# Six reordered places and two shares for GpSimd in a transformer kernel: picks by products at the start of its expert layer

## The chip, the cores and the metric

The kernel runs on one core of a Trainium2 chip, as one program. The metric is the device time of one execution in microseconds, the median of several runs. TensorE does the matrix products (PE in the profile), VectorE (DVE) and ScalarE (ACT) the elementwise work, GpSimd (POOL) a small part of it and the indirect transfers, and SyncE (SP) issues transfers. ScalarE issues transfers too.

## The reference, cut to what matters

The input is 256 latent tokens and 256 context tokens of width 2048, all in float32. The first block has four layers (Fourier mixing, mLSTM, attention, Fourier mixing); each normalizes, projects, mixes, projects back and adds. The second block is a sparse attention with 16 heads beside a pooling branch, and then a layer of 16 experts in 4 groups:

```python
def _moe_sublayer(x, ffn_norm_g, ...):
    ht = _rms(x, ffn_norm_g).reshape(B * S, D)
    g_prob = softmax(ht @ w_router_group + b_router_group)
    p_group, g_sel = lax.top_k(g_prob, 1)                  # one group of experts for each token
    e_logit = (ht @ w_router_expert + b_router_expert)[that group]
    top_val, top_idx = lax.top_k(e_logit, 2)               # two experts of the group
    w_top = softmax(top_val) * p_group
    ...
    for e in range(N_EXPERTS):
        hid = silu(ht @ w_expert_gate[e]) * (ht @ w_expert_up[e])
        y = y + combine[:, e:e + 1] * (hid @ w_expert_down[e])
    return x + y
```

## The kernel before

**Products in three parts.** Every float32 operand is split into a high part (a rounded copy, `WH` for weights and `HTH`, in the code `HH_`, for activations) and a low part (the rest, `WL` and `HTL`, in the code `HL_`). Each product is three matmuls: high by high, low by high, high by low. The weights come in pieces of 128 x 1024, some 700 in all, by a ring of five raw slots `WR` (in the expert layer seven more in `SCB` and `YT`). A piece is cut in two steps: ScalarE writes the high part (L1369, in `cut_to`), VectorE the low part (L2060). There are three slots for cut pieces, so cut number s waits until TensorE has used piece s − 3. ScalarE, and from the last Fourier layer on SyncE, issues the load of the next piece into a raw slot once its low part is cut (`wfree`). `along(job)` cuts, at the place in the program where a job is treated, the pieces that should be ready by then; `ahead(job)` says how far.

**Order.** Each engine runs a program of its own in a fixed order (`tensor_program`, `scalar_program`, and those of VectorE, GpSimd and SyncE); between them stand semaphore waits on named events such as `("x", tag, n)` (block n of the residual is updated), `("sq", tag, n)` (squared), `("lo", s)` (piece s is cut). An engine that waits holds up all that is behind in its program.

**Layers.** `outproject` handles the 16 output blocks of a layer: TensorE fills a bank, VectorE adds it to x (L2040), ScalarE squares it (L1456), and VectorE sums x and squares. After block 15, `sums_of` (L605, L606) adds over the partitions by products with a column of ones, ScalarE takes the root (L1385), which needs its Sqrt table (ACT_TABLE_LOAD), VectorE the reciprocal, and `rows_from` (L613) spreads it over the partitions; then the first blocks of the next layer are scaled. `kproject` (L561 to L563) runs a piece of weights over four banks at a time; with tag 2 it makes the first four output blocks of the attention layer. `gainnorm` on VectorE scales the last normalized x for the sparse attention, in the order cut, product `mo`, low part. At the end of the last Fourier layer (tag 3) and of the sparse attention ("nsa"), `split_y` writes the high (L1462, ScalarE) and low part (L2031, VectorE) of 16 blocks for the output product. Lines L491 to L493 and L512 to L514 are output and input products with 256 or 512 columns.

**Expert layer.** After block 15 of x, the router's logits are known; VectorE picks the groups, TensorE counts (L1232 to L1235), and VectorE writes the one-hot matrix `E_P` from token to sorted slot, 5 tiles of 128 slots (L2037). `tokens` (L1243) turns it into token numbers; GpSimd gathers the rows of x from HBM in sorted order (`gather_part`, `gather`, L3402), which `rows_out` stored before (L1483, L3490). TensorE transposes them (`turn_rows`, L1215), ScalarE and VectorE split them (`rows_in`), and the gate_up jobs `("gu", s, x)` run (L1269 to L1271), 8 pieces each, followed by down jobs `("dn", s)` (L1291) in the order of `down_order`. `late_5` computes scales (L3187) that the matmuls of `scales` (L1252) turn into slot order. `finish` adds a down block to x before GpSimd scatters it.

## Time and profile before

| | |
|---|---|
| median of three runs | 3165.92 us (3161.19 to 3166.24) |
| the profiled execution's own time | 3163.28 us |
| its span, first to last instruction | 3161.5 us |
| mean granted TensorE clock | 0.983 |
| busy: TensorE / VectorE / ScalarE / GpSimd | 3058.8 / 2156.6 / 1290.4 / 154.4 us |
| HBM read / written | 627.14 / 15.73 MB |

Times in rows are microseconds from the start of the span. A timeline row gives start, duration, engine, line of the kernel, instruction, out<-in, shapes, and, in brackets, how long the engine had been idle and what ended this. Rows of matmuls overlap. The chain that ended last consists of TensorE to 85%, VectorE to 8% and ScalarE to 4%.

### The profile page before, as it was taken

The page shows a single profiled execution, that of the slowest core. Times are in us where ns is not written, and L with a number is a line of the kernel's source. Part 1 is how long each engine was busy: PE and PEld are TensorE (multiplying, and loading weights), DVE is VectorE, ACT ScalarE, POOL GpSimd, SP SyncE. Part 2 cuts the span into 40 slices and gives each one's busy share as a digit, 9 for nine tenths or more (in the row PEclk, how much of TensorE's full clock was granted, in tenths as well). Part 3 has the DMA queues.
Part 4 walks back from the last instruction along what each step waited for, and adds up shares of the span by engine and source line. Part 5 has one row for each costly group of instructions (what it writes and reads, how often), then busy time and mean ns, then how long its engine had stood idle before and what let it go on. Part 6 is the DMA issues. An engine that isn't in the chain of part 4 may idle for free.

```text
span 3161.5 us, 44203 instructions
## 1 busy us (share of the span) xinstructions
PE 3058.8 (97%) x17432; PEld 2578.3 (82%) x17432; DVE 2156.6 (68%) x3774; ACT 1290.4 (41%) x2068; POOL 154.4 (5%) x237
## 2 busy tenths in 40 slices
PE   7999999999999999999999999999999999979998
PEld 5777777788888888878777879999899988967776
DVE  4576875778788665676568855665756676556897
ACT  3322324422232232332445554444444454435676
POOL 0000001000000000000100000000101200010011
PEclk8999999999999999999999999999999999989999
DMA  8778783355455545467367635456664434576897
GB/s 315 275 269 291 276 297 127 124 176 171 155 189 169 178 164 179 142 214 245 119 203 251 227 124 193 148 174 201 206 216 139 153 136 155 178 267 204 301 371 273
DMA packets 191007, 647.87 MB, mean 205 GB/s; under 512 B 21952, under 2 KB 30272, under 8 KB 190416
## 3 DMA queue, kind: packets, MB, share of 16 engines
q1 hardware_dynamic: 126656, 416.88, 38.2%
q10 hardware_dynamic: 59184, 211.31, 19.6%
q0 software_dynamic: 4960, 16.85, 1.6%
q8 instruction: 137, 2.24, 0.3%
q14 instruction: 70, 0.57, 0.1%
HBM read 627.14 MB, written 15.73 MB: 203 GB/s over the span
## 4 chain that ended last, share of the span: by engine, by line
PE 85%; DVE 8%; ACT 4%; DMA 1%; issue 1%; SPq 0%; ACTq 0%; POOL 0%; POOLq 0%; DVEq 0%
PE PS L491 14%; PE PS L493 13%; PE PS L492 13%; PE PS L588 7%; PE PS L590 7%; PE PS L589 7%; DVE WL L2060 3%; ACT WH L1369 2%; PE PS L1269 2%; PE PS L883 2%; PE PS L668 2%; PE PS L1271 2%; PE PS L1270 2%; DVE AR L2040 1%; DMA AR<-ada_p 1%
## 5 line engine op out<-in xcount | busy, mean ns | idle before, releaser
L2060 DVE TENSOR_TENSOR WL<-WR,WH 128x1024 fp32r<-128x1024 f32 (+1 forms) x646 | 778.9, 1212 | 518.2 <-ACT WH L1369 515.1
L1369 ACT ACTIVATE WH<-WR 128x1024 fp32r<-128x1024 f32 (+1 forms) x646 | 672.1, 1046 | 992.6 <-PE PS L493 528.5
L491 PE MATMUL PS<-HTH,WH 128*128 128x256 f32 (+1 forms) x2656 | 883.8, 333 | 4.9 <-DVE WL L2060 4.9
L493 PE MATMUL PS<-HTH,WL 128*128 128x256 f32 (+1 forms) x2656 | 870.1, 328 | 0.0
L492 PE MATMUL PS<-HTL,WH 128*128 128x256 f32 (+1 forms) x2656 | 870.0, 328 | 0.0
L491 PEld LDWEIGHTS PS<-HTH,WH 128*128 128x128 f32 x2656 | 505.7, 190 | 71.3 <-issue 22.3
L492 PEld LDWEIGHTS PS<-HTL,WH 128*128 128x128 f32 x2656 | 505.9, 190 | 44.0 <-issue 1.7
L493 PEld LDWEIGHTS PS<-HTH,WL 128*128 128x128 f32 x2656 | 505.7, 190 | 43.8
L588 PE MATMUL PS<-WH,HTH 128*128 128x512 f32 x1016 | 408.4, 402 | 3.8 <-DVE WL L2060 3.8
L590 PE MATMUL PS<-WH,HTL 128*128 128x512 f32 x1016 | 396.4, 390 | 0.0
L589 PE MATMUL PS<-WL,HTH 128*128 128x512 f32 x1016 | 395.7, 389 | 0.0
L588 PEld LDWEIGHTS PS<-WH,HTH 128*128 128x128 f32 x1016 | 190.9, 188 | 46.7 <-DVE WL L2060 6.1
L589 PEld LDWEIGHTS PS<-WL,HTH 128*128 128x128 f32 x1016 | 191.0, 188 | 40.8 <-issue 3.3
L590 PEld LDWEIGHTS PS<-WH,HTL 128*128 128x128 f32 x1016 | 190.7, 188 | 40.8
L2082 DVE CUSTOM_DVE_ANT_0 WR<-WR,SCB,MOD 128x1024 f32<-128x1024 f32 x128 | 164.2, 1283 | 13.7 <-DMA WR<-ada_w 10.0
L2082 DVE CUSTOM_DVE_ANT_0 WR<-WR,SCB 128x1024 f32<-128x1024 f32 x128 | 156.5, 1223 | 14.6 <-DMA WR<-ada_w 11.0
L1269 PE MATMUL PS<-WH,HTH 128*128 128x512 f32 x320 | 130.6, 408 | 3.2 <-DVE WL L2060 1.7
L1271 PE MATMUL PS<-WH,HTL 128*128 128x512 f32 x320 | 126.9, 397 | 0.0
L1270 PE MATMUL PS<-WL,HTH 128*128 128x512 f32 x320 | 126.8, 396 | 0.0
L2060 DVE TENSOR_TENSOR WL<-YT,WH 128x1024 fp32r<-128x1024 f32 x80 | 97.0, 1223 | 24.4 <-ACT WH L1369 22.2
L1369 ACT ACTIVATE WH<-YT 128x1024 fp32r<-128x1024 f32 x80 | 84.9, 1061 | 38.3 <-PE PS L1271 30.0
L2040 DVE SCALAR_TENSOR_TENSOR YT<-PS,MOD,YT 128x256 f32<-128x256 f32 x96 | 43.3, 481 | 81.4 <-PE PS L493 77.6
(429 smaller groups left out, 3933.4 us busy)
## 6 DMA issues: line engine op xcount, KB each, us to landing
WR<-ada_w SPq DMA_DIRECT2D x256, 512.0 KB, 4.6
AR<-ada_p SPq DMA_DIRECT2D x64, 512.0 KB, 6.6
AR<-ada_p ACTq DMA_DIRECT2D x64, 512.0 KB, 6.2
WR<-m_vo ACTq DMA_DIRECT2D x64, 512.0 KB, 4.4
WR<-a_qz ACTq DMA_DIRECT2D x64, 512.0 KB, 4.6
WR<-n_m SPq DMA_DIRECT2D x64, 512.0 KB, 4.1
WR<-e_gu SPq DMA_DIRECT2D x53, 512.0 KB, 5.4
YT<-e_gu SPq DMA_DIRECT2D x51, 512.0 KB, 5.9
```

The lines of the kernel that those rows point to most:

```text
L491: e.matmul(ps[:, 0:n], wh[:, k, :], xh, start=c == 0, stop=False)
L492: e.matmul(ps[:, 0:n], wh[:, k, :], xl, start=False, stop=False)
L493: i = e.matmul(ps[:, 0:n], wl[:, k, :], xh, start=False, stop=c == K - 1)
L588: e.matmul(ps[:], HH_[:, c, t], wh[:, k, :], start=c == 0, stop=False)
L589: e.matmul(ps[:], HH_[:, c, t], wl[:, k, :], start=False, stop=False)
L590: i = e.matmul(ps[:], HL_[:, c, t], wh[:, k, :], start=False, stop=c == 15)
L1269: e.matmul(ps[:], hi[:, t], wh[:, k, :], start=c == 0, stop=False)
L1270: e.matmul(ps[:], hi[:, t], wl[:, k, :], start=False, stop=False)
L1271: m = e.matmul(ps[:], lo[:, t], wh[:, k, :], start=False, stop=c == 15)
L1369: e.activation(part_of(WH, s), place_of(plan["slot"][p])[:, 0:width(s)], ACT.Copy, scale=1.0).then_inc(*L.up(hi_done, ("hi", s)))
L2060: e.tensor_tensor(part_of(WL, s), place_of(plan["slot"][plan["split"][s]])[:, 0:width(s)], part_of(WH, s).bitcast(F32), ALU.subtract).then ...
L2082: e.tensor_tensor_reduce(out=o, in0=x, in1=SCB[:, v, k], scale=1.0, scalar=m if half else 0.0, op0=ALU.mult, op1=ALU.add, accum_out=m).the ...
```

## The change

Nine edits, lettered for what follows; the arithmetic is the same in all but M.

- **A** `kproject`, tag 2: pieces 0 and 1 are run over banks 0 and 1 first, then over banks 2 and 3.
- **B** `outproject`: `along` of block 15 stands behind the last x update (VectorE) and behind the last square (ScalarE); `sums_of` runs the products of the sums before it waits for the last square.
- **C** `gainnorm` for "nsa": pending low parts are made ahead of a cut.
- **D** Last Fourier layer: ScalarE's root for `GE` and one cut more stand ahead of splits 12 to 15; GpSimd writes the low parts of odd blocks below 12.
- **E** Sparse attention, first pair of heads: a cut stands ahead of each of the four halves, not of the first head's two.
- **F** End of the sparse attention: one cut between split 7 and 8, the router weights' multiply in pair 6, low parts of odd blocks below 8 by GpSimd.
- **M** Start of the expert layer: the Sqrt table is loaded at block 14 and the root stands right behind the sums; the rows of the first four chunks are made by products of x (`TX`, in SBUF) with the one-hot matrix (`pick_rows`); parts are gathered in the order 1, 2, 3, 0; slot 5 of the raw ring, the later gathers, and SyncE's further loads wait for other events.
- **S** `late_5` at piece 6, not 7.
- **G** `down_order(3)` takes three blocks at a time, with `finish` at steps 11 to 13.

```diff
@@ down_order @@
-            return [(b, x) for bs in ((0, 1), (2,), (3,)) for xs in ((0, 1, 2), (3,)) for b in bs for x in xs]
+            return [(b, x) for bs in ((0, 1, 2), (3,)) for xs in ((0, 1, 2), (3,)) for b in bs for x in xs]
+    def on_pool(tag, n):
+        return n % 2 == 1 and n < {3: 12, "nsa": 8}.get(tag, 0)
@@ TensorE, kproject @@
+            def columns(q, s, ms):
...
+            if tag == 2:
+                pieces = weights(("out4",), [sources[n] for n in range(8)])
+                for q in range(2):
+                    columns(q, pieces[q], (0, 1))
+                for q, s in enumerate(pieces):
+                    columns(q, s, (2, 3) if q < 2 else (0, 1, 2, 3))
+                    if q in between:
+                        between[q]()
+                return
@@ TensorE, sums_of @@
-            w.wait_ge(L.at(("sum", tag, 14), ("sq", tag, 15)))
+            w.wait_ge(L.at(("sum", tag, 14)))
             for tb in range(n // 128):
+                e.matmul(ps[:, tb:tb + 1], r[:, 128 * tb:128 * tb + 128], ONE[:, 0:1], start=tb == 0, stop=False)
+            w.wait_ge(L.at(("sq", tag, 15)))
...
@@ TensorE, moe @@
+            def pick_rows(p):
+                ps = wrk(("xg", 0, p))
+                w.wait_ge(L.at(("P", 0), *(("rowx", 2 * p + c) for c in range(2))))
+                for c in range(2):
+                    at = 128 * (2 * p + c)
+                    for tb in range(2):
+                        m = e.matmul(ps[:, 256 * c:256 * c + 256], TX[:, tb, at:at + 128],
+                                     E_P[tb][:, 0:2, :].rearrange("p t n -> p (t n)").bitcast(F32), start=tb == 0, stop=tb == 1)
+                m.then_inc(*L.up(mm_done, ("full", ("xg", 0, p)), *(["picked"] if p else [])))
             for p in range(2):
-                turn_rows(0, p)
+                pick_rows(p)
@@ ScalarE, outproject @@
-                if n < NB and (tag != 2 or n >= 4):
+                if n < NB - 1 and (tag != 2 or n >= 4):
                     along(("out", tag, n))
                 if n >= lag:
                     square(tag, n - lag, sq)
+                if n == NB:
+                    along(("out", tag, NB - 1))
+                if tag == "nsa" and n == 14:
+                    e.activation(E_RT, EPSC[:].to_broadcast([128, 2]), ACT.Sqrt, scale=1.0).then_inc(*L.up(act_done))
+                if tag == "nsa" and n == NB:
+                    w.wait_ge(L.at(("full", ("stat", "nsa"))), L.last(act_done))
+                    e.activation(E_RT, place[("stat", "nsa")][:, 0:2], ACT.Sqrt, ...)
@@ ScalarE, fnet end @@
-            for n in range(12, NB):
-                split_y(tag, n, cols, [])
             if tag == 3:
                 w.wait_ge(L.at("ge2"))
                 e.activation(GE, GE, ACT.Sqrt, bias=EPSC[:], scale=1.0).then_inc(*L.up(act_done, "ge"))
+                cut_to(plan[("out", tag, 0)][0] + NP + 1)
+            for n in range(12, NB):
+                split_y(tag, n, cols, [])
@@ ScalarE and VectorE, nsa @@
-                        if h == 0:
+                        if p == 0:
                             cut_to(cut[0] + 1)
...
-            go(99)
+            go(1)
             for n in range(NB):
+                if n == 8:
+                    cut_to(cut[0] + 1)
+                    go(1)
                 split_y("nsa", n, LAT, [("full", ("n_m", 1, 15))])
@@ VectorE, outproject @@
-                    along(job)
+                    if n < NB - 1:
+                        along(job)
...
+                if n == NB - 1:
+                    along(job)
@@ VectorE, gainnorm @@
+                if j >= 6 and j % 2 == 0:
+                    for x in late:
+                        low(x)
+                    late.clear()
                 keep_up(tag, j)
@@ VectorE, moe @@
-            late = {0: [late_0], 1: [late_1], 2: [indices, addresses], 3: [late_2], 4: [late_3], 5: [late_4], 7: [late_5]}
+            late = {0: [late_0], 1: [late_1], 2: [indices, addresses], 3: [late_2], 4: [late_3], 5: [late_4], 6: [late_5]}
...
-                    if phase == ("dn", 3) and q in (8, 9, 13):
-                        finish(3, (8, 9, 13).index(q))
+                    if phase == ("dn", 3) and 11 <= q < 14:
+                        finish(3, q - 11)
@@ GpSimd @@
+        def split_y(tag):
+            for n in range(NB):
+                if on_pool(tag, n):
+                    w.wait_ge(L.at(("yh", tag, n)))
+                    e.tensor_tensor(HL_[:, n, 256:512], YT[:, n, 256:512], HHF[:, n, 256:512], ALU.subtract).then_inc(
+                        *done(("ys", tag, n)))
...
-            for b in range(4):
+            for b in (1, 2, 3, 0):
                 for t in range(2):
                     gather_part(t, b)
+            w.wait_ge(L.at("picked"))
             for t in range(2, 5):
                 gather(t)
@@ SyncE and the plan of slots @@
-                w.wait_ge(L.at(("row", 0, 0)))
+                w.wait_ge(L.at(("row", 0, 1)))
                 load_pieces()
-        here, newest = {}, {}
+        here, newest = {}, {R: -0.5}
...
-                                     ("rows", "stored") if s < R + 2 else "x_dead")
+                                     "picked" if s == R else ("rows", "stored") if s < R + 2 else "x_dead")
```

## Rows read from the trace of the kernel before

**Rows 1.** The page: span, and busy time, share of the span and instructions of TensorE.

```profile
span 3161.5 us, 44203 instructions
...
PE 3058.8 (97%) x17432; PEld 2578.3 (82%) x17432; DVE 2156.6 (68%) x3774; ACT 1290.4 (41%) x2068; POOL 154.4 (5%) x237
```

**Rows 2.** TensorE's table of waits: us in total, times, longest us.

```profile
PE PS L605 <- ACT AR L1456: 7.4, 4, 2.4
PE PS L1215 <- DMA AR<-xtok,SML: 7.3, 1, 7.3
...
PE PS L512 <- DVE WL L2060: 5.1, 3, 2.3
PE PS L491 <- DVE WL L2060: 4.9, 2, 4.6
PE PS L561 <- DVE YT L2040: 4.4, 1, 4.4
...
PE PS L561 <- DVE HTL L2031: 3.1, 5, 0.7
```

**Rows 3.** Windows: us, busy (instructions) of five engines, granted clock, DMA share, GB/s.

```profile
1878.04:1882.47 4.43, 4.43 (x24) 4.43 (x25) 1.66 (x3) 0.00 (x0) 0.00 (x0) 0.61 0.01 4
2408.00:2414.70 6.70, 4.13 (x19) 4.16 (x20) 4.63 (x9) 2.38 (x4) 0.00 (x0) 0.50 0.44 136
2773.20:2793.50 20.30, 9.35 (x29) 7.57 (x30) 8.69 (x26) 4.51 (x7) 7.68 (x8) 0.50 0.69 235
```

**Rows 4.** VectorE's timeline: start, us, instruction [idle before <-releaser].

```profile
1877.47 0.42 DVE L2040 SCALAR_TENSOR_TENSOR YT<-YT,PS 128x256 f32<-128x256 f32 x1
```

**Rows 5.** ScalarE's timeline at the first transition.

```profile
517.19 0.63 ACT L1456 ACTIVATE AR<-YT 128x512 f32<-128x512 f32 x1 [4.77 <-DVE YT L2040]
...
519.92 0.26 ACT L1385 ACTIVATE RT<-PS,EPSC 128x4 f32<-128x4 f32 x1 [0.80 <-PE PS L606]
```

**Rows 6.** The page's groups: xcount | busy, mean ns | idle before, releaser.

```profile
L2060 DVE TENSOR_TENSOR WL<-WR,WH 128x1024 fp32r<-128x1024 f32 (+1 forms) x646 | 778.9, 1212 | 518.2 <-ACT WH L1369 515.1
L1369 ACT ACTIVATE WH<-WR 128x1024 fp32r<-128x1024 f32 (+1 forms) x646 | 672.1, 1046 | 992.6 <-PE PS L493 528.5
```

**Rows 7.** VectorE's timeline in the norm of the sparse attention.

```profile
2222.22 1.23 DVE L2060 TENSOR_TENSOR WL<-WR,WH 128x1024 fp32r<-128x1024 f32 x1 [1.43 <-ACT WH L1369]
...
2226.00 1.23 DVE L2060 TENSOR_TENSOR WL<-WR,WH 128x1024 fp32r<-128x1024 f32 x1 [1.43 <-ACT WH L1369]
```

**Rows 8.** VectorE's timeline at the last Fourier layer's end.

```profile
2118.09 2.36 DVE L2060 TENSOR_TENSOR WL<-WR,WH 128x1024 fp32r<-128x1024 f32 x2 [1.78 <-ACT WH L1369]
```

**Rows 9.** GpSimd's groups by form, whole span.

```profile
L3284 POOL TENSOR_TENSOR HTL<-AR,HTH 128x256 fp32r<-128x256 f32 x32 | 26.2, 821 | 571.9 <-ACT AR L1406 571.9
```

**Rows 10.** VectorE's timeline at the sparse attention's end.

```profile
2668.69 0.49 DVE L2031 TENSOR_TENSOR AR<-AR,SML 128x320 f32<-128x320 f32 x1
```

**Rows 11.** ScalarE's timeline at the start of the expert layer.

```profile
2769.67 0.38 ACT L1483 ACTIVATE SCB<-PS 128x256 f32<-128x256 f32 x1 [0.97 <-PE PS L656]
2770.07 1.28 ACT L1952 ACT_TABLE_LOAD   x1
```

**Rows 12.** TensorE's timeline at the same place.

```profile
2777.16 1.01 PE L1243 MATMUL PS<-M_CS,HTL 128*128 128x2 f32 x4 [2.86 <-DVE HTL L2037]
...
2788.11 0.77 PE L1269 MATMUL PS<-WH,HTH 128*128 128x512 f32 x1 [0.75 <-issue]
...
2793.37 0.72 PE L1215 MATMUL PS<-IDN,AR 128*128 128x128 f32 x4
```

**Rows 13.** TensorE's groups by form, 2450 to 2700.

```profile
L1095 PE MATMUL PS<-SCB,WR 128*128 128x256 f32 x64 | 16.9, 385 | 0.0
```

**Rows 14.** SyncE's queue at the same place.

```profile
2777.36 11.77 SPq L3451 DMA_DIRECT2D YT<-e_gu  x5
```

**Rows 15.** TensorE's timeline, two stalls of the expert layer.

```profile
2817.74 2.40 PE L1252 MATMUL PS<-SML,HTL 128*128 128x5 f32 x20 [1.45 <-DVE SML L3187]
...
3138.47 0.47 PE L1291 MATMUL PS<-WH,HTH 128*128 128x512 f32 x1 [1.54 <-DVE HTL L2031]
```

More of the change, by code:

```diff
@@ L544, in kproject @@
             banks = []
-            for q, s in enumerate(weights(("out4",) if tag == 2 else ("first", tag), [sources[n] for n in range(8)])):
+            def columns(q, s, ms):
+                wh = WH[:, ws(s), :].rearrange("p (k n) -> p k n", n=512)
+                wl = WL[:, ws(s), :].rearrange("p (k n) -> p k n", n=512)
+                w.wait_ge(L.at(("lo", s)))
+                for m in ms:
+                    if q == 0:
+                        banks.append(acc(jobs[m]))
+                    ps, n = banks[m][:, 0:b - a], slice(128 * m, 128 * m + 128)
+                    for k in range(2):
+                        c = 2 * q + k
+                        w.wait_ge(L.at((ready, tag, c)))
+                        e.matmul(ps, wh[:, k, n], HH_[:, c, a:b], start=c == 0, stop=False)
+                        e.matmul(ps, wh[:, k, n], HL_[:, c, a:b], start=False, stop=False)
+                        i = e.matmul(ps, wl[:, k, n], HH_[:, c, a:b], start=False, stop=c == 15)
+                if ms[-1] == 3:
+                    i.then_inc(*L.up(mm_done, ("used", s), *([("full", job) for job in jobs] if q == 7 else [])))
+            if tag == 2:
[7 more added lines that the diff above has]
+                return
+            for q, s in enumerate(weights(("first", tag), [sources[n] for n in range(8)])):
                 wh = WH[:, ws(s), :].rearrange("p (k n) -> p k n", n=512)
@@ L550, in kproject @@
                     banks = [acc(job) for job in jobs]
-                if q == 0 and ready == "h":
+                if q == 0:
                     i = first_piece(tag, 0, [ps[:, 0:b - a] for ps in banks],
@@ L554, in kproject @@
                                     lambda H, c, m: H[:, c, a:b], lambda c, m: high(tag, c), 15)
-                for m in range(0 if q or ready != "h" else 4, 4):
+                for m in range(0 if q else 4, 4):
                     n = slice(128 * m, 128 * m + 128)
@@ L601, in sums_of @@
             r = RS if n == 512 else RA
[L602 removed]
+            w.wait_ge(L.at(("sum", tag, 14)))
             for tb in range(n // 128):
[L604 to L606 removed]
+                e.matmul(ps[:, tb:tb + 1], r[:, 128 * tb:128 * tb + 128], ONE[:, 0:1], start=tb == 0, stop=False)
+            w.wait_ge(L.at(("sq", tag, 15)))
+            for tb in range(n // 128):
+                i = e.matmul(ps[:, tb:tb + 1], SQR[1][:, 128 * tb:128 * tb + 128], ONE[:, 0:1], start=False,
+                             stop=tb == n // 128 - 1)
             i.then_inc(*L.up(mm_done, ("full", ("stat", tag))))
@@ L1476, in outproject @@
                     square(tag, n - lag, sq)
+                if n == NB:
[4 more added lines that the diff above has]
+                    w.wait_ge(L.at(("full", ("stat", "nsa"))), L.last(act_done))
+                    e.activation(E_RT, place[("stat", "nsa")][:, 0:2], ACT.Sqrt, bias=EPSC[:], scale=1.0 / 2048).then_inc(
+                        *L.up(act_done, ("root", "nsa"), ("free", ("stat", "nsa"))))
                 if n >= lag and tag == "nsa":
@@ L1950, in moe @@
         def moe():
-            w.wait_ge(L.at(("full", ("stat", "nsa"))))
-            e.activation(E_RT, place[("stat", "nsa")][:, 0:2], ACT.Sqrt, bias=EPSC[:], scale=1.0 / 2048).then_inc(
-                *L.up(act_done, ("root", "nsa"), ("free", ("stat", "nsa"))))
             def rows_in(s, p):
@@ L3037, in nsa @@
                 pair_out(p)
+                if p == 6:
+                    w.wait_ge(L.at("r_w", "gains"))
+                    by_20 = E_RW.rearrange("p (c n) -> p c n", c=16)
+                    tt(by_20, by_20, GN[:, 32:48].rearrange("p (c n) -> p c n", n=1).to_broadcast([128, 16, 20]), ALU.mult,
+                       "r_wg")
                 if p < 7:
@@ L3044, in nsa @@
                     go(2)
-            go(99)
+            go(1)
             for n in range(8):
                 split_y("nsa", n, LAT)
+            cut_to(cut[0] + 1)
+            go(1)
             gated(7)
@@ L3222, in finish @@
             def finish(s, b):
-                w.wait_ge(L.at(("full", ("dn", s, b))))
+                w.wait_ge(L.at(("full", ("dn", s, b)), ("row", s, b)))
                 for i, t in enumerate(TILES[s]):
@@ L3493, in sync_program @@
                 w.wait_ge(L.at("ord"))
-                passed.update(("x_dead", ("rows", "stored")))
+                passed.update(("x_dead", ("rows", "stored"), "picked"))
                 group.append(e.value_load(E_ORD[0:1, 0:1], min_val=0, max_val=3))
```

12 lines of the change are left out of this document (5 added, 7 removed).

## The prediction

> **What bounds the kernel now.** I read the page's busy shares first: TensorE works 3058.8 of 3161.5 us, 97% [rows 1], so the idle time to be won is 103 us in the whole span. The second view is TensorE's table of waits: no single wait is over 8 us, and the edits aim at six of its rows, which hold 32.2 us between them [rows 2], and at two smaller waits of the expert layer. The third is the granted clock in the stretches behind those waits: it reads 0.50, which is 1.2 in place of 2.4 GHz, for 6.7 us around the first heads of the sparse attention and for 20.3 us at the start of the expert layer, and 0.61 on the mean of the piece behind the stall of 4.4 us [rows 3]. So a wait costs its own length and something more, while the matmuls behind it run at the lower level. The work of TensorE itself is left nearly as it is, so the gain is the waits that go, less the waits that come.
>
> Everything goes by the times of the profiled execution, whose 3163.28 us are 2.64 below the median of 3165.92; only the difference is carried over to the median.
>
> **The change part by part.**
>
> **A, first output blocks of the attention layer (kproject, tag 2).** TensorE waits 4.4 us for the last two of four accumulator banks [rows 2]; they come free at about 1877.9, by the row at 1877.47 [rows 4]. Only two banks are wanted first now, and these were freed earlier. Two pieces by two blocks are 24 matmuls, as many as the piece that took 4.43 us at a clock of 0.61 [rows 3]; at full clock 0.61 x 4.43 = 2.7 to 2.9 us, which fit into the stall. The stall keeps some 0.7 for the fourth bank, and what the low clock costs behind it (4.43 − 2.8 = 1.6) goes. Against it: the next scores wait for ScalarE, whose table load of 1.28 us now starts when TensorE is already further on; I give back 0.6. −3.7 − 1.6 + 0.6 = −4.7; bounds −2.7 (the clock stays down) and −6.1.
>
> **B, ends of four layers.** The cut (split of the next weight pieces) belonging to the last block is moved behind the last x update on VectorE and behind the last square on ScalarE. There TensorE waits 7.4 us in all for that square [rows 2]. The sums no longer wait for it in one go: the first matmuls of each pair run ahead, which is worth up to 0.9 where four pairs run. But two cuts now lie between the last square and the root. In the first transition the square ends at 517.82, the table load follows, and the root starts at 519.92 [rows 5]. After: two cuts of 1.05 (ScalarE), between them VectorE's 1.22 for the low part [rows 6], for which the next load's issue waits on ScalarE, then the table load: 517.8 + 1.05 + 1.22 + 0.34 + 1.28 = 521.7, +1.9 with the gaps. Nothing covers this: TensorE, VectorE and the next layer's first block all wait for the root. The second transition is the same, +1.9. In the third ScalarE issues no load, and VectorE reaches x a little earlier: +1.3. In the fourth no table is loaded and the x update isn't held up by square sums: −0.4. Sum +4.7, and as idle time grows ahead of matmuls that run at half clock anyhow, I add 0.8: +5.5. Bounds: −1.5 (the cuts were needed there at once anyway, so that the work is only moved, and the split sums gain), +9.7 (each transition loses both cuts in full on both engines, 2 x 1.05 + 2 x 1.22 = 4.5 twice, +0.7).
>
> **C, norm of the sparse attention.** VectorE's loop repeats every 3.78 us (2222.22, 2226.00), each time idle 1.43 for ScalarE's cut [rows 7]; TensorE waits 3.1 us in five times [rows 2]. In the loop lies one low part of 0.42, queued behind the cut; flushed ahead of it, it leaves the chain. Four stalls of 0.67 shrink by 0.6, the first by 0.4: −2.9; bounds −1.5, −3.3.
>
> **D, last Fourier layer.** The longest of the weight stalls at L512 [rows 2]: TensorE waits 2.3 us for a low part that VectorE starts at 2118.09, after 1.78 idle for ScalarE [rows 8]. ScalarE's cut of that piece moves ahead of four splits, so that VectorE starts at about 2116.3: −1.8. GpSimd takes six odd low parts at 0.82 us each [rows 9]; VectorE's own take 0.34 to 0.42, but it waits for ScalarE at that place, so this buys nothing. It could cost: six by 0.82 end up to 1.2 us behind the blocks that use them. Bounds −3.7, +0.8.
>
> **E, first heads of the sparse attention.** TensorE's 4.6 us for a weight piece [rows 2], with half clock for 6.7 us of which 4.13 are busy [rows 3], a loss of 2.05. Four cuts now lie in the first two heads in place of two, each 1.22 in VectorE's queue ahead of masks and sums. Followed, the third piece is there 3.8 earlier (stall 0.8), the fourth stalls 1.1 and the fifth 3.0: 4.9 of stall for 4.6, and the lost clock comes back only in part (−1.5): −1.2. Bounds −4.6, +1.
>
> **F, end of the sparse attention.** The router's multiply of 0.49 goes from VectorE's queue [rows 10] to an earlier pair with slack, four of eight low parts go to GpSimd, and one cut is put between the halves. Of the 5.1 us that L512 waits for weights [rows 2] about 2.2 lie here. The piece behind them is cut some 5 us sooner; the fourth then limits, and the job ends 3.2 us earlier: −3.2. Bounds −4.7, and +1 if GpSimd's last low part, four by 0.82 = 3.3 us after its first, is late.
>
> **M, start of the expert layer.** The Sqrt table is loaded two blocks sooner and the root stands ahead of a copy: 0.38 and 1.28 leave the chain [rows 11], −1.7. The Square behind the early load needs no other table: at the fourth transition the root follows a Square with no load between. Then the tokens of the first two pairs are picked by products with the one-hot matrix, not gathered and transposed. TensorE waits 7.3 us for that gather [rows 2]. The picks can start when the token matmuls end, 2777.16 + 1.01 − 1.7 = 2776.5 [rows 12]. They are eight float32 matmuls of 256 columns; the nearest row is the pool's, two records for each such matmul, 16.9 / 64 = 0.264 us a record [rows 13], so 16 records are 4.2 us at 2.4 GHz and 8.4 at 1.2. With the lower level for most of it, as the clock row shows there, I take 7.1: 2783.6. The first piece takes 5.3 us at half clock (2788.11 to 2793.37, [rows 12]), at full clock at best half of that, 2.6; I take 2.85; its low rows and weights are ready by 2783. Ending at 2786.6 and not 2793.4 it gains 6.8, with the 1.7 in it: −6.8. Bounds: half clock throughout, 2776.5 + 8.4 + 5.3 = 2790.2, −3.2; full, with the rows as limit, −7.5.
>
> The Trainium skill, "ScalarE: Activation LUTs", section "What ACT_TABLE_LOAD costs", gives 1.28 us for the load and some 1.38 for a drain, 2.66 in all. The row has the load's 1.28 and a start 0.02 us after the copy before it, so no drain is seen here; by the page this term would be 1.38 larger.
>
> **S and G.** The late scales are made one piece sooner: the stall of 1.45 at 2817.74 [rows 15] goes, −1.4 (0, −3). In the last group the down blocks run three wide: the stall of 1.54 at 3138.47 [rows 15] gets two more pieces ahead of it, but the finishing updates are bunched at the end: −1.2 (+0.5, −1.5).
>
> Sum: −4.7 + 5.5 − 2.9 − 1.8 − 1.2 − 3.2 − 6.8 − 1.4 − 1.2 = −17.7; 3165.9 − 17.7 = 3148.
>
> **The rivals.**
> 1. *The ends of layers cost nothing* (B at 0): the cuts moved behind the root's chain were wanted early and give back elsewhere what they take. For it: VectorE idles 515 us in all ahead of low parts for ScalarE's cuts [rows 6], so order is loose. Against: the root has nothing ahead of it but these. 3148.2 − 5.5 = 3143.
> 2. *GpSimd is late.* Its 0.82 [rows 9] is twice VectorE's. If next to VectorE's cuts it goes to 1.7, D and F are lost and turn into waits of a microsecond each: 3148 + 5 + 2 = 3155. The Trainium skill, "GPSIMD Engine Reference", sections 1 and 4.1, says that the engine shares its interfaces to SBUF with VectorE and is about twice as slow on two inputs; the rows agree on the second, the first is untried in them.
> 3. *Weights are late at the expert layer.* SyncE issues five loads over 11.8 us there [rows 14]. The loads behind the first three now wait for another gathered block; if the fourth piece comes no earlier than now, 4.6 of the 6.8 are given back at the fourth piece: 3153.
> 4. *Edits cancel* (chains that end as late by another wait): within 6 us of before, 3163.
> 5. *Slower: the low clock lasts.* With the stall split up, the clock stays at 1.2 GHz through the picks and the first job. Against it: it rose 5.4 us into the first piece. Price: the first piece and picks +3.6; the 24.4 us from 2793.4 to the stall at 2817.7 [rows 15] become 1.85 times as long (5.3 for my 2.85 a piece), +20.7; 3148.2 + 24.3 = 3172.5. It cancels the gain from 16.6 us at the lower level, and reaches slower from the full 24.
>
> **How the numbers follow.** The forecast has 0.45, the rivals in turn 0.20, 0.12, 0.13, 0.06 and 0.04. The range is 3138 to 3161: rivals 1 to 3 lie in it, and the bounds of B and M, taken together, reach it. No change means within 0.2% or 6.3 us, about what a measurement can tell. Faster 0.83, same 0.12, slower 0.05.
>
> **What would show it.** A: TensorE's 4.4 us on YT falls under 1. B: the four L1385 roots come 1 to 2 us later behind their squares. C: the wait on HTL under 1 in all. M: no wait on the gathered tokens, and the first piece's end 6 to 7 us nearer to the last x update. E is the weakest: I expect more, smaller waits. The prediction is wrong if B's cuts turn out hidden, if GpSimd shows times over 1.2 us, or if the clock in the picks stays at 0.50 into the second piece.

## The result

The changed kernel takes 3146.17 us (median of five runs, 3141.49 to 3147.17), the kernel before 3165.67 us beside it; the ratio is 0.994, with a 95% interval of 0.9927 to 0.9952. The forecast was 3148. The two executions with a trace, 3163.28 and 3147.17, are 16.1 us apart; the medians are 19.5 apart, as the traced execution of before lies 2.4 under its median and that of the changed kernel 1.0 over its own.

The page of the changed kernel, its span and the engines' busy time. TensorE is busy for 2.3 us more than before [rows 1], in a span that is 16.1 us shorter:

```profile
span 3145.4 us, 44227 instructions
...
PE 3061.1 (97%) x17440; PEld 2580.8 (82%) x17440; DVE 2157.7 (69%) x3764; ACT 1290.5 (41%) x2069; POOL 165.0 (5%) x247
```

TensorE's table of waits of the changed kernel (us in total, times, longest). It answers to [rows 2]; L637 is L605 of before for the squares, L645 is L613 (row statistics spread over the partitions), L494 is L491, L515 is L512:

```profile
PE PS L645 <- DVE RT L2097: 11.7, 4, 3.3
...
PE PS L494 <- DVE WL L2111: 5.2, 4, 3.0
PE PS L515 <- DVE HTL L2082: 4.0, 3, 2.4
...
PE PS L637 <- ACT AR L1498: 3.3, 4, 0.9
...
PE PS L515 <- DVE WL L2111: 0.9, 2, 0.6
```

Two rows of the table of before that the argument needs:

```profile
PE PS L512 <- DVE HTL L2031: 3.0, 3, 1.3
...
PE PS L613 <- DVE RT L2046: 2.5, 4, 0.7
```

Of the rows of before, the gather (7.3) and the norm of the sparse attention (3.1) are gone, the banks (4.4) are down to 0.7, and L512's weights (5.1) to 0.9. Others have moved. The wait for squares fell from 7.4 to 3.3, but the one behind it, for the row statistics, grew from 2.5 to 11.7 us in the same four times: together 9.9 before and 15.0 now. L512's wait for low parts grew from 3.0 to 4.0. And the wait of L491 for weights was 4.9 in 2 times and is 5.2 in 4.

**The time, stretch by stretch.** The k-th matmul of TensorE can be laid beside the k-th matmul of the other trace (8 places later behind the picks), so the difference of two start times tells what has been gained up to there. Worked out from the two traces, at places of the changed kernel in us:

```
stretch                                     after - before   forecast
0 to 140      start                             +1.9            0
140 to 1500   B, first layer's end              +2.3          } 
1500 to 1860  B, second                         +1.7          } +5.5 with the fourth
1970 to 2095  B, third                          +1.5          }
1860 to 1970  A                                 -4.2          -4.7
2095 to 2195  D                                 -0.1          -1.8
2195 to 2385  B, fourth, and C                  -4.5          (-0.4) and -2.9
2385 to 2650  E                                 +0.4          -1.2
2650 to 2758  F                                 -3.4          -3.2
2758 to 2797  M                                 -9.3          -6.8
2797 to 2830  S                                 -1.3          -1.4
2830 to 3110  no edit                           +0.6            0
3110 to end   G                                 -1.7          -1.2
sum                                            -16.1         -17.7
```

Most terms were near, but that the sum is as near as this is in part luck: D and E fell short by 3.3 us together, and M and the row of C gave 3.7 more than forecast. Single terms are read with care: the clock alone moves some stretches by 1.5 us between two traces (below).

**B in the trace.** ScalarE at the first layer's end, in the changed kernel. It answers to [rows 5]:

```profile
519.09 0.63 ACT L1498 ACTIVATE AR<-YT 128x512 f32<-128x512 f32 x1 [10.02 <-DVE YT L2091]
...
519.62 1.99 ACT L1411 ACTIVATE WH<-WR 128x1024 fp32r<-128x1024 f32 x2
...
522.32 1.28 ACT L1427 ACT_TABLE_LOAD   x1 [0.71 <-DVE WL L2111]
...
523.61 0.26 ACT L1427 ACTIVATE RT<-PS,EPSC 128x4 f32<-128x4 f32 x1
```

Between the square and the table load stand two cuts and then 0.71 us in which ScalarE waits for VectorE's low part, since the issue of the next load needs it. From the square's start to the root's are 4.52 us, before they were 519.92 − 517.19 = 2.73 [rows 5]: +1.8, with +1.9 forecast. TensorE's wait for the statistics at that place:

```profile
524.14 2.07 PE L645 MATMUL PS<-IDN,RT 128*128 128x128 f32 x8 [3.32 <-DVE RT L2097]
```

Both waits of an end together, for the last square and for the statistics, grew by 1.87, 1.87 and 1.80 us at the first three ends, 5.5 in sum. At the fourth the root comes 1.0 us sooner behind its square (2.19 us, before 3.23), but TensorE has little of it. VectorE there, in the changed kernel and then in the one before:

```profile
2208.65 2.36 DVE L2111 TENSOR_TENSOR WL<-WR,WH 128x1024 fp32r<-128x1024 f32 x2 [1.89 <-ACT WH L1411]
2210.93 0.17 DVE L2097 RECIPROCAL RT<-RT 128x4 f32<-128x4 f32 x1
```

```profile
2208.65 0.18 DVE L2046 RECIPROCAL RT<-RT 128x4 f32<-128x4 f32 x1 [4.18 <-ACT RT L1388]
```

The root starts at 2209.47 in the one and at 2208.21 in the other. Two low parts of cuts now stand ahead of the reciprocal and hold it until 1.46 us behind the root's start, where it was 0.44. What ScalarE gains there, VectorE gives back.

**M in the trace.** TensorE at the start of the expert layer, which answers to [rows 12]:

```profile
2770.34 1.02 PE L1285 MATMUL PS<-M_CS,HTL 128*128 128x2 f32 x4 [2.86 <-DVE HTL L2088]
2771.22 5.44 PE L1256 MATMUL PS<-HTL,SCB 128*128 128x256 f32 x16
2776.54 0.47 PE L1311 MATMUL PS<-WH,HTH 128*128 128x512 f32 x1
...
2779.39 0.60 PE L1247 MATMUL PS<-IDN,AR 128*128 128x128 f32 x4
```

The picks (L1256) start as soon as the tokens' products end, there is no wait behind them, and the first piece lasts 2779.39 − 2776.54 = 2.85 us. Windows of the same place (us, busy (instructions) of five engines, granted clock, DMA share, GB/s):

```profile
2768.00:2772.00 4.00, 1.66 (x6) 1.57 (x7) 2.65 (x16) 0.00 (x0) 0.00 (x0) 0.50 0.37 103
2772.00:2774.00 2.00, 2.00 (x6) 1.55 (x6) 0.35 (x2) 1.02 (x1) 1.27 (x2) 0.50 0.95 379
2774.00:2776.00 2.00, 2.00 (x9) 1.69 (x8) 1.31 (x2) 1.06 (x4) 1.70 (x2) 0.81 0.90 352
2776.00:2780.00 4.00, 4.00 (x21) 3.15 (x20) 3.93 (x6) 2.48 (x4) 3.09 (x4) 1.00 0.62 200
```

The clock is back at 2.4 GHz within the picks, before the first piece. Before it stayed at 0.50 through the 20.3 us up to 2793.5 [rows 3].

### The profile page after: what moved, and what is told of

It is laid out like the page before. It is cut to its first block, busy times and chain, and to the rows that moved or that the text cites. A ratio compares the mean times of both kernels' runs of the same rounds, so it can differ in the third digit from the quotient of the medians.

```text
span 3145.4 us, 44227 instructions
## 1 busy us (share of the span) xinstructions
PE 3061.1 (97%) x17440; PEld 2580.8 (82%) x17440; DVE 2157.7 (69%) x3764; ACT 1290.5 (41%) x2069; POOL 165.0 (5%) x247
## 4 chain that ended last, share of the span: by engine, by line
PE 86%; DVE 7%; ACT 4%; issue 1%; DMA 1%; SPq 0%; POOL 0%; ACTq 0%; POOLq 0%; DVEq 0%
PE PS L494 14%; PE PS L496 13%; PE PS L495 13%; PE PS L618 7%; PE PS L620 7%; PE PS L619 7%; DVE WL L2111 3%; PE PS L1311 2%; PE PS L915 2%; ACT WH L1411 2%; PE PS L1313 2%; PE PS L1312 2%; PE PS L700 2%; DMA AR<-ada_p 1%; PE PS L973 1%
## 5 line engine op out<-in xcount | busy, mean ns | idle before, releaser
L494 PE MATMUL PS<-HTH,WH 128*128 128x256 f32 (+1 forms) x2656 | 884.3, 333 | 5.2 <-DVE WL L2111 5.2
L494 PEld LDWEIGHTS PS<-HTH,WH 128*128 128x128 f32 x2656 | 505.6, 190 | 72.0 <-issue 21.8
```

Source lines behind the costliest of these rows:

```text
L494: e.matmul(ps[:, 0:n], wh[:, k, :], xh, start=c == 0, stop=False)
```

## The experiments

All kernels are the changed one with the edit shown. "Place" is the difference to the changed kernel in the stretch of the edit, "from 140 us" that from there to the last matmul, both by the comparison of matmuls above. The medians differ from that of the changed kernel by −4.5 (no_pool), −9.6 (b_early), −2.5 (no_e) and +3.7 us (no_pick), each 1.6 to 4.2 us lower than its "from 140 us". The reference trace is the slowest execution of the changed kernel, 1.0 us over its median, and the first 140 us differ from trace to trace; that these two make up the whole of it is not shown.

### no_pool: GpSimd makes no low parts

```diff
-        return n % 2 == 1 and n < {3: 12, "nsa": 8}.get(tag, 0)
+        return n % 2 == 1 and n < {}.get(tag, 0)
```

> Takes GpSimd's shares of D and F away: VectorE makes all 16 low parts at both places. Theory (GpSimd and VectorE slow one another: VectorE's low parts take 0.80 us beside it and 0.34 alone, its cut 1.75 and 1.23): 12 low parts in 4.1 us and not 6 in 4.8; the stall of 2.38 us at the end of the last Fourier layer falls to 1.3 or less, at the end of the sparse attention 0.5 goes; the time falls by 1.5 to 2.5 us, to 3144. Rival (the share relieves VectorE, as six and four fewer of its instructions would say): 2 to 3 us more, 3149.

3141.66 us (3140.01 to 3142.1), ratio to before 0.9927 (0.991 to 0.9943). Place: −1.7 in D, −0.5 in F; from 140 us −2.9. The changed kernel at the end of the last Fourier layer, on VectorE, on GpSimd, and on TensorE:

```profile
2108.41 4.80 DVE L2082 TENSOR_TENSOR HTL<-YT,HTH 128x256 fp32r<-128x256 f32 x6
2113.14 1.75 DVE L2111 TENSOR_TENSOR WL<-WR,WH 128x1024 fp32r<-128x1024 f32 x1
```

```profile
2108.66 5.15 POOL L3397 TENSOR_TENSOR HTL<-YT,HTH 128x256 fp32r<-128x256 f32 x6 [123.54 <-ACT HTH L1504]
```

```profile
2119.62 0.58 PE L515 MATMUL PS<-HTH,WH 128*128 128x256 f32 x1 [2.38 <-DVE HTL L2082]
```

And without the share, on VectorE and on TensorE:

```profile
2106.01 4.11 DVE L2082 TENSOR_TENSOR HTL<-YT,HTH 128x256 fp32r<-128x256 f32 x12
2110.24 1.23 DVE L2111 TENSOR_TENSOR WL<-WR,WH 128x1024 fp32r<-128x1024 f32 x1
```

```profile
2116.19 0.38 PE L515 MATMUL PS<-HTH,WH 128*128 128x256 f32 x1 [1.35 <-DVE HTL L2082]
```

VectorE makes twelve low parts alone in 4.11 us, and six in 4.80 while GpSimd makes the other six. Halving its work made it slower, 0.80 us each and not 0.34, with no idle time over 0.1 us between them; the cut behind them grew from 1.23 to 1.75, and the stall of TensorE from 1.35 to 2.38. The theory held, the rival fell. Of the −1.7 in D, 1.0 is this stall. The other 0.7 is matmuls at a lower clock behind it: the two traces of the changed kernel and that of no_e have them, and those of no_root and b_all, where GpSimd has its share as well, do not. So the share costs 1.0 us at this place for certain, and up to 1.7.

### pool_twice: GpSimd makes all of them

```diff
-        return n % 2 == 1 and n < {3: 12, "nsa": 8}.get(tag, 0)
+        return n < {3: 12, "nsa": 8}.get(tag, 0)
```

> Doubles the suspected cost of D and F: GpSimd makes all 12 low parts at the end of the last Fourier layer and all 8 of the first half at the end of the sparse attention, not the odd ones. Theory (GpSimd takes 0.82 us for one however free VectorE is, and slows VectorE while it runs): 12 take 9.8 us or more and not 4.1, TensorE waits for them; VectorE's next cut beside it takes 1.7 us in place of 1.2; the end of the last Fourier layer is 3 to 6 us later, that of the sparse attention 2 to 4. Rival (GpSimd's 0.86 us were caused by VectorE alone, and with VectorE idle it takes half): 12 in 5 to 6 us, within 1 us of the changed kernel.

One execution, 3144.99 us. Place: +0.3 in D, where +3 to +6 was expected, and +3.2 in F, where 2 to 4 was. GpSimd's twelve low parts, then the first seven of them, then the seventh and eighth:

```profile
2104.12 9.43 POOL L3397 TENSOR_TENSOR HTL<-YT,HTH 128x256 fp32r<-128x256 f32 x12 [123.23 <-ACT HTH L1504]
2104.12 4.90 POOL L3397 TENSOR_TENSOR HTL<-YT,HTH 128x256 fp32r<-128x256 f32 x7 [123.23 <-ACT HTH L1504]
2108.27 2.41 POOL L3397 TENSOR_TENSOR HTL<-YT,HTH 128x256 fp32r<-128x256 f32 x2
```

VectorE beside it, and TensorE at the same place:

```profile
2108.38 1.72 DVE L2111 TENSOR_TENSOR WL<-WR,WH 128x1024 fp32r<-128x1024 f32 x1 [4.13 <-ACT WH L1411]
...
2111.32 2.57 DVE L2082 TENSOR_TENSOR YT<-AR 128x129 f32<-128x129 f32 x4
```

```profile
2110.73 0.58 PE L515 MATMUL PS<-HTH,WH 128*128 128x256 f32 x1 [1.04 <-POOL HTL L3397]
```

With VectorE idle GpSimd takes 4.90 / 7 = 0.70 us for one low part, and beside VectorE's low parts 5.15 / 6 = 0.86. Beside VectorE's cut it loses more: the eighth is drawn out to 1.7 us, and the same happens at the end of the sparse attention (1.70 us at 2658.30). VectorE loses too: that cut takes 1.72 us and not 1.23, and four sums of 128 x 129 take 2.57 us beside GpSimd and 1.02 to 1.03 without it. So both engines lose; beside low parts VectorE loses the larger share (0.5 us each, GpSimd 0.16), beside a cut GpSimd does (1.0 us against 0.5). The expectation for D was wrong: TensorE waits 1.04 us for GpSimd's low parts, with a clock of 0.67 behind it, but the wait of 2.38 us for VectorE's later ones does not come. This kernel is ahead of the first trace of the changed one all the same: by 3.1 us at 140 us, and by two stretches of 1.5 us that are told of below.

### b_early: the first three layers' ends as before

```diff
-                if n < NB - 1 and (tag != 2 or n >= 4):
+                if n < NB - (tag not in EARLY) and (tag != 2 or n >= 4):
                     along(("out", tag, n))
...
-                if n == NB:
+                if n == NB and tag not in EARLY:
                     along(("out", tag, NB - 1))
...
-                    if n < NB - 1:
+                    if n < NB - 1 or tag in EARLY:
                         along(job)
...
-                if n == NB - 1:
+                if n == NB - 1 and tag not in EARLY:
                     along(job)
...
+    EARLY = (0, 1, 2)
```

> Undoes a part of B: in the ends of the first three layers the cut of the last block stands ahead of the x update and of the last square again; the split sums stay. Theory (the two cuts lie on the chain square, root, next layer): the first three roots come 1.8, 1.8 and 1.5 us sooner, the low clock behind them costs less, and the time falls by 5 to 6 us, to about 3140.5. Rival 1 (the cuts give elsewhere what they take here): within 1 us of 3146.2.

3136.54 us (3134.62 to 3138.56), ratio 0.9914 (0.9897 to 0.993). Place: −2.1, −3.1 and −1.6 at the three ends; 1.4 of it comes back further on, from 140 us −5.4. The trace's start is ahead by 6.6 us more (below); whether the other executions' starts are, and make up the rest of the −9.6 of the medians, is not shown. ScalarE at the first end:

```profile
512.54 0.63 ACT L1500 ACTIVATE AR<-YT 128x512 f32<-128x512 f32 x1 [4.78 <-DVE YT L2093]
513.19 1.28 ACT L1429 ACT_TABLE_LOAD   x1
514.88 0.26 ACT L1429 ACTIVATE RT<-PS,EPSC 128x4 f32<-128x4 f32 x1 [0.41 <-PE PS L639]
```

From square to root 2.34 us: the 4.52 are gone, and with the split sums kept it is 0.4 less than the 2.73 of before. Rival 1 of the prediction, that the cuts were wanted at once and cost nothing there, is refuted; the cuts stood on the chain and were hidden where they stood before.

### b_all: B undone whole

The edit of b_early with a longer list, which takes in the end of the sparse attention too, and the wait of the sums:

```diff
+    EARLY = (0, 1, 2, 3, "nsa")
...
-            w.wait_ge(L.at(("sum", tag, 14)))
+            w.wait_ge(L.at(("sum", tag, 14), ("sq", tag, 15)))
```

> Undoes B whole: all five ends of layers, and the split sums. Theory: as b_early at the first three ends, but with the root waiting for all eight (four) products behind the square, some 0.2 us later than in b_early at each, since a root now waits for four products and not for the table load; at the fourth end 0.8 to 1 us more than the changed kernel, where the x update is held up by the cut and the square sums. Rival (the fourth end gains nothing by the move): no difference there.

One execution, 3138.55 us; from 140 us −7.7. Place: −2.6, −1.8 and −1.6 at the first three ends, −0.1 where the fourth end and C lie. 1.7 of the −2.6 come at 620 to 630 us, where nothing was edited. So the split sums' worth can't be read from these sums, 6.0 here and 6.8 in b_early. At the roots it can: from square to root it takes 2.72, 2.72 and 1.73 us here, and 2.34, 1.94 and 1.73 in b_early, so they bring the root forward by 0.4, 0.8 and 0.0. At the fourth end the theory fell: TensorE waits 3.10 us in all there, 3.08 in b_early and in again, where the cut is moved, and 2.62 in the first trace of the changed kernel. The move gains nothing sure, by the reciprocal told of above. At the end of the sparse attention, the fifth, TensorE's waits are the same with and without the move (1.68 and 2.86 us).

### no_e: the cuts of the first heads as before

```diff
-                        if p == 0:
+                        if h == 0:
                             cut_to(cut[0] + 1)
```

> Undoes E: a cut ahead of the first head's two halves only. Theory (E exchanges one wait of 4.6 us for three of 0.9, 0.9 and 3.0, and the low clock comes later, not less): the time falls by 0.4, within the noise, at 3145.8, and the one wait of 4.6 us is back. Rival (E gains, as a stall of 4.6 us that goes should): 1 to 2 us more.

3143.68 us (3142.46 to 3145.03), ratio 0.9935 (0.9919 to 0.9952). Place: −0.7; from 140 us +0.3. E moves nothing that can be told from chance. TensorE's waits in the changed kernel there, and then the one without E:

```profile
2405.44 0.35 PE L494 MATMUL PS<-HTH,WH 128*128 128x256 f32 x1 [0.87 <-DVE WL L2111]
...
2409.46 0.39 PE L494 MATMUL PS<-HTH,WH 128*128 128x256 f32 x1 [0.92 <-DVE WL L2111]
...
2415.62 0.36 PE L494 MATMUL PS<-HTH,WH 128*128 128x256 f32 x1 [3.03 <-DVE WL L2111]
```

```profile
2406.05 0.36 PE L494 MATMUL PS<-HTH,WH 128*128 128x256 f32 x1 [4.58 <-DVE WL L2111]
```

4.82 us of wait in three places take the place of 4.58 in one.

### no_pick: gather and transposes as before, early root kept

```diff
-                pick_rows(p)
+                turn_rows(0, p)
...
-            for b in (1, 2, 3, 0):
+            for b in range(4):
...
-            w.wait_ge(L.at("picked"))
...
-                passed.update(("x_dead", ("rows", "stored"), "picked"))
+                passed.update(("x_dead", ("rows", "stored")))
...
-                w.wait_ge(L.at(("row", 0, 1)))
+                w.wait_ge(L.at(("row", 0, 0)))
...
-        here, newest = {}, {R: -0.5}
+        here, newest = {}, {}
...
-                                     "picked" if s == R else ("rows", "stored") if s < R + 2 else "x_dead")
+                                     ("rows", "stored") if s < R + 2 else "x_dead")
```

> Undoes the picks by products in M: the first four chunks are gathered and transposed as before, with the gather order, slot order and waits of before; the early Sqrt table and root stay. Theory (root 2.0 us, picks 7.3 us of the 9.3 that the start of the expert layer gained): the time rises by 7.3, to 3153.5, and TensorE waits some 7.3 us for the gathered tokens again. Rival (the clock explains most: with picks TensorE works through and is at 2.4 GHz for the first piece): the same total, but split as about 4.5 us of wait and 2.5 us of slower first piece.

3149.85 us (3147.44 to 3153.27), ratio 0.9952 (0.9935 to 0.9968). Place: +6.3; from 140 us +7.0. TensorE:

```profile
2778.88 1.94 PE L1247 MATMUL PS<-IDN,AR 128*128 128x128 f32 x8 [7.54 <-DMA AR<-xtok,SML]
2781.57 0.77 PE L1311 MATMUL PS<-WH,HTH 128*128 128x512 f32 x1 [0.76 <-DVE HTL L2091]
...
2785.94 0.60 PE L1247 MATMUL PS<-IDN,AR 128*128 128x128 f32 x4
```

The wait of 7.54 is back. The tokens' products start at 2770.32 here and at 2770.34 in the changed kernel; the first piece ends at 2785.94 and 2779.39, 6.6 us apart. Of these the piece itself is 4.37 − 2.85 = 1.5, which is the clock (0.62 from 2781.5 to 2786.0 here, 1.00 in the changed kernel); the other 5 are the wait (7.54) and the transposes with their splits (2781.57 − 2778.88 = 2.7) less the picks (5.3). The rival's split, 4.5 of wait and 2.5 of clock, is nearer than the theory, whose 7.3 was the wait alone. The median rose by only 3.7 us; the traced execution is the slowest of its four.

### no_root: Sqrt table and root where they were

```diff
-                if tag == "nsa" and n == 14:
-                    e.activation(E_RT, EPSC[:].to_broadcast([128, 2]), ACT.Sqrt, scale=1.0).then_inc(*L.up(act_done))
-                if tag == "nsa" and n == NB:
-                    w.wait_ge(L.at(("full", ("stat", "nsa"))), L.last(act_done))
-                    e.activation(E_RT, place[("stat", "nsa")][:, 0:2], ACT.Sqrt, ...)
...
         def moe():
+            w.wait_ge(L.at(("full", ("stat", "nsa"))))
+            e.activation(E_RT, place[("stat", "nsa")][:, 0:2], ACT.Sqrt, ...)
```

> Undoes the early Sqrt table and the early root of M alone; picks stay. Theory (the load of 1.28 and the copy of 0.38 stand on the chain that leads to the picks): 2.0 us more at the start of the expert layer. Rival (the picks wait for the stored rows or for something else than the root): less than 0.5 us more.

One execution, 3148.37 us. Place: +3.0; from 140 us +1.5. TensorE waits 3.65 us for the first counts there and 1.68 in the changed kernel: 2.0 by the wait. The counts and the picks behind it took 0.4 us more each, at the low clock, and 0.3 is a wait for low rows further on.

### no_g: the last down blocks as before

```diff
-            return [(b, x) for bs in ((0, 1, 2), (3,)) for xs in ((0, 1, 2), (3,)) for b in bs for x in xs]
+            return [(b, x) for bs in ((0, 1), (2,), (3,)) for xs in ((0, 1, 2), (3,)) for b in bs for x in xs]
...
-                    if phase == ("dn", 3) and 11 <= q < 14:
-                        finish(3, q - 11)
+                    if phase == ("dn", 3) and q in (8, 9, 13):
+                        finish(3, (8, 9, 13).index(q))
```

> Undoes G. Theory (G removes the wait for the last hidden blocks wholly, 1.5 us, and the finishing updates in the tail are not longer): 1.7 to 2.4 us more, all of it in the last 25 us. Rival (the gain there came with the earlier parts of the change): under 1 us.

One execution, 3150.96 us. Place: +1.7, all in the last 40 us, where the stall of 1.5 us is back:

```profile
3126.15 0.47 PE L1333 MATMUL PS<-WH,HTH 128*128 128x512 f32 x1 [1.52 <-DVE HTL L2082]
```

### again: the changed kernel unaltered

> The changed kernel unaltered, to see how much of a difference between two traces is chance. Theory (the first 140 us, with their loads and low clock, differ by several us from one execution to the next, and the rest by under 1): 3144 to 3147, the trace off by up to 4 us at 140 us and by under 1 us more behind it. Rival (the start is fixed by the kernel): the same start to 0.3 us.

3145.47 us (3140.39 to 3147.31), ratio 0.9934 (0.9919 to 0.9949). At 140 us it is 0.5 us ahead of the first trace of the same kernel, and from there to the end it loses 0.6, by one wait of 0.63 us at 2787 us that the first trace lacks. So two executions can agree to 0.6 us over 3000, as the theory said; its differences of several us at 140 us did not come. Each is the slowest of its set, though, and the nine executions of this kernel lie between 3140.39 and 3147.31. Where the faster ones gain is not shown. The traces of the other kernels, whose engines run the same operations in the same order in the first 140 us, differ there by more. Windows of the first 140 us (columns as above), of the changed kernel in this second trace and then of b_early:

```profile
0.00:140.00 140.00, 115.85 (x934) 81.79 (x935) 57.39 (x140) 46.00 (x102) 5.83 (x20) 0.90 0.86 319
```

```profile
0.00:140.00 140.00, 116.67 (x960) 83.12 (x961) 63.41 (x152) 49.27 (x108) 5.83 (x20) 0.94 0.87 323
```

b_early has 26 matmuls more behind it at 140 us, at a clock of 0.94 and not 0.90, and is 6.6 us ahead; nothing was edited there. The offsets at 140 us to the first trace of the changed kernel run from −6.6 to +1.1 in the ten traces of altered kernels; the kernel before stands at −1.9. Whether this start belongs to an execution or to a build stays open.

### best and best_2: what pays, together

best is b_early, no_pool and no_e in one. best_2 has no_pool, all five ends of layers as before (the split sums stay), and keeps E.

> The changed kernel without what the runs showed to cost: the cut ahead of the last square again in the first three layers (as in b_early), no share for GpSimd (as in no_pool), E undone (as in no_e). Theory (the three are apart in time and add): read from 140 us on, 5.5 + 2.5 + 0.5 us less than the changed kernel, ratio to the kernel before 0.991, about 3137 where before is 3165; the rival (b_early's 3136.5 owes some to a start that was fast by chance, and the terms overlap): 3139 to 3141.

> As best, but with all five ends of layers as before the change (the split sums stay) and with E kept. Theory (neither E nor the fourth end moves the time): the same as best to 1 us, ratio 0.990. Rival (the fourth end did gain by the move, as 0.8 us in the trace of the changed kernel seemed to say): 1 us more than best from 140 us on.

best: 3133.91 us (3131.63 to 3136.35), ratio 0.9903 (0.9887 to 0.992); from 140 us −10.0 against the changed kernel, where 8.5 was expected; 1.7 of the −10.0 come at 620 to 630 us, where nothing was edited. best_2: 3136.32 us (3133.07 to 3139.8), ratio 0.9913 (0.99 to 0.9927); from 140 us −10.8. The two can't be told apart by their intervals, so neither the fourth end nor E shows an effect. Either is faster than the changed kernel: every execution of the two is below every one of its nine, though the interval of best_2 touches its 0.9927 to 0.9952.

**Chance in the rest of the trace.** Some stretches without an edit differ by 1.5 us between two traces. Behind the stall of 3.03 us in the sparse attention, the changed kernel and then pool_twice, which is edited elsewhere. Both windows end at the same place of the program, within a matmul; the second begins 1.45 us before the matmul at which the first begins, inside the stall:

```profile
2415.60:2425.00 9.40, 9.38 (x67) 9.35 (x68) 4.55 (x7) 2.60 (x5) 3.61 (x4) 0.82 0.63 204
```

```profile
2410.80:2420.20 9.40, 7.95 (x68) 7.92 (x69) 6.07 (x9) 3.93 (x7) 4.48 (x4) 1.00 0.62 198
```

The granted clock is 0.82 in the one and 1.00 in the other. One low stretch costs or spares 1.5 us (−1.49 for pool_twice here, −1.55 for it between 560 and 1500 us). The instructions of the stretch don't settle whether it comes: no_pool has 1.00 here like pool_twice, but best_2, which has no share for GpSimd either, has 0.82. The changed kernel has 0.82 in both its traces, so whether it belongs to an execution or to a build stays open. That is the grain: a total of one trace says nothing below 1.5 us, and only single waits and durations, most of which repeat to 0.1 us, say more.

## Why the prediction was right

The total, 3148 against 3146.17, is in the range, and the direction and most of the mechanisms are as forecast. In the traces it is −18.0 from 140 us on, for a forecast of −17.7, with errors of up to 2.5 us a term that cancel. By its steps:

- **A**: −4.7 forecast, −4.2 measured. The wait of 4.4 is 0.67 now; the give-back is one wait of 0.70 for ScalarE. Right.
- **B**: +5.5 forecast, +5.5 at the first three ends alone (2.3 + 1.7 + 1.5), as TensorE's waits there give too (1.87 + 1.87 + 1.80). The root's delay was +1.8 for a forecast of +1.9, and b_early gives the time back. The third end was priced at +1.3 and cost as much as the others, and the 0.8 added for idle time was not needed; the two errors cancel. The step on the fourth end (−0.4) can't be told from zero, as b_all shows: it did not count the reciprocal, which now waits for VectorE's moved low parts. "Up to 0.9" for the split sums held (0.4, 0.8 and 0.0 us at the three roots).
- **C**: −2.9 forecast (its own terms, 4 x 0.6 + 0.4, give 2.8); with the fourth end −4.5 in place, of which 3.3 come at 2220 to 2240 us, where the norm is, and TensorE's 3.1 us on this row are gone from the table. Not tried by itself, so its split from the fourth end is argued.
- **D**: −1.8 forecast, −0.1 measured. The step that failed is "this buys nothing" for GpSimd's share, with VectorE's duration taken from the row without a neighbour. The reordering alone gives its −1.8: with no_pool, D stands −0.1 − 1.7 = −1.8 against before, and the wait for weights falls from 2.32 us to 0.45. The share costs the 1.7, of which 1.0 is a longer wait and 0.7 a lower clock that not every trace has. The two-sided bound (+0.8) held. Rival 2 named the mechanism in part: it had GpSimd late, and in the changed kernel it was VectorE that slowed, while GpSimd's low parts took 0.72 to 0.93 us. The 1.7 us beside VectorE's cut that it feared came in pool_twice.
- **E**: −1.2 forecast, +0.4 measured, not told from zero by no_e. The three waits of 0.8, 1.1 and 3.0 followed came out as 0.87, 0.92 and 3.03. What failed is the 1.5 of clock credited on top: the low clock moved behind the third wait. In no_pool and pool_twice it does not come there, and the stretch is 1.5 us shorter; so the credit is there in some traces and not in others.
- **F**: −3.2 forecast, −3.4 measured, in spite of a share that costs 0.5.
- **M**: −6.8 forecast, −9.3 measured. The mechanism is right and the term was undersized: the picks took 5.3 us, not 7.1, as the clock rose while they ran and not at their end, and the root gained 2.0 by its wait, not 1.7, since the wait behind the copy went too. The measured value lies outside the term's own bounds (−3.2 to −7.5): the bound had the first piece limited by its low rows and weights, ready by 2783, but it started at 2776.54, which is 2781.0 in the times of the trace before (4.4 us lie between the traces at 2758 us). A small slip is in the sum too: 2783.6 + 2.85 is 2786.45, not 2786.6. The parts add up: about 2 to 3 for the root (no_root) and 6.3 for the picks (no_pick).
- **S**: −1.4 forecast, −1.3 measured. **G**: −1.2 forecast, −1.7 measured, by no_g 1.7: the wait went wholly and the finishing updates cost nothing.

Of the rivals, the late weights at the expert layer (3) did not come: TensorE waits 1.7 us in five times for the weights of the gate_up jobs, as before. The low clock that lasts (5) did the opposite. The change holds two parts that harm (B's moved cuts at three ends, GpSimd's shares), one with no effect that can be told from chance (E), and others that help: from 140 us on it gained 18.0 us, and best, without the three, gained 28.0.

## What to carry to other kernels

Before a piece of hidden work is moved, ask which chain it will stand in: cuts of 1 to 2 us that were free ahead of a wait cost TensorE 1.8 to 1.9 us of waiting behind it, at each of three places. At the fourth the move freed one engine's step and held up another's, and gained nothing sure. Work given to a second engine should be counted with what it does to the first one's instructions, not only with its own duration; six of twelve taken away made the other six take longer than all twelve. And lay two traces side by side instruction by instruction, so that the terms show apart from a start that differs by more than most of them. Stretch totals of single traces still carry 1.5 us of chance by the clock; a wait that comes back when the edit is undone is the better evidence.

## What the runs showed that was not expected

- VectorE's subtraction of two 128 x 256 operands takes 0.34 us alone and 0.80 us beside the same operation on GpSimd; a cut of 128 x 1024 takes 1.23 and up to 1.75. GpSimd's takes 0.70 alone, 0.86 beside VectorE's, and 1.7 beside VectorE's cut. The Trainium skill, "GPSIMD Engine Reference", section 1 "Specifications", says that GpSimd shares its SBUF interfaces with VectorE and contends with VectorE's instructions that have two SBUF inputs; these rows agree, and they show that both engines lose.
- The first 140 us of a span differ by up to 7.7 us (−6.6 to +1.1) between traces of kernels that run the same operations there, with a granted clock of 0.90 to 0.94. Two traces of one kernel differ by 0.5.
- A low stretch of the clock behind the same stall comes in one trace and not in another, and is worth 1.5 us.
